# Moving the sample heads' means, two pieces of GpSimd's work and a table load inside one stage of a hybrid recurrent decoder step

## The chip, the cores and the metric

The kernel runs on one core of one Trainium2 chip, as a single launch. The metric is the time of that launch in microseconds on the device, taken as the median of several runs. TensorE is called PE here, VectorE DVE, ScalarE ACT, GpSimd POOL and SyncE SP, as in the profile. Each engine works through its own list of instructions in order; between engines there are only semaphores.

## The reference, cut to what matters

Two layers run over 320 tokens: a prompt of 256 and 8 samples of 8 tokens. Each layer is a SwiGLU feed-forward, a mixer, and a second feed-forward, with a layer norm after each. Half of the mixer's columns go to RWKV-7 heads, half to four mLSTM heads. The change lies in the mixer, where these two pieces meet:

```python
# mLSTM, per chunk of a sequence: C is the matrix memory, n the normaliser
num = g_inter[..., None] * jnp.einsum('bhtd,bhde->bhte', qc, C) + jnp.einsum('bhts,bhse->bhte', s, vc)
den = g_inter * jnp.einsum('bhtd,bhd->bht', qc, n) + s.sum(-1)
h = num / jnp.maximum(jnp.abs(den), jnp.exp(-m_t))[..., None]
C = dec[..., None, None] * C + jnp.einsum('bhs,bhsd,bhse->bhde', ws, kc, vc)
...
mu = h.mean(-1, keepdims=True)
var = jnp.mean(jnp.square(h - mu), -1, keepdims=True)
h = ((h - mu) * lax.rsqrt(var + MH_EPS)).reshape(B, T, D_B).astype(dt) * mh_g

# RWKV-7, per token: S is the matrix state
S = (S * w_t[:, :, None, :] + sa[..., None] * (kk_t * a_t)[:, :, None, :]
     + v_t[..., None] * k_t[:, :, None, :])
```

## The kernel before

The RWKV recurrence is done in chunks of 64 tokens: four of the prompt and one that holds all samples. Each chunk needs the inverse of a triangular matrix, which is grown in doublings. The stage that does this has 27 **steps** (`NSTEP`), numbered n, each a pair of a doubling level and a chunk. In a step PE makes a product, DVE masks it into `t1` (L1726, "the mask of step n"), PE makes the growth from it (L764 and L767), and ACT copies the growth back (L1183). After the last step the recurrence over the chunks begins, which needs every growth.

The mLSTM heads' work is threaded through the same 27 steps by hand: lists of step numbers say after which step each engine does which piece (`SIDE_AT`, `WEIGHTS_AT`, `NUMS_OUT_AT`, `SQUARES_AT`, `ROOTS_AT` for ACT; `PRODUCTS_AT`, `MEANS_AT`, `SPREADS_AT`, `SCALED_AT` and `LEFT_AT` for DVE; `LEFT_AT` for PE as well). There is no planner. What an engine has listed first it does first, and waits at it if it has to.

The pieces that the change and the prediction touch:

- `own_queries` (L1474, DVE): four products of two tiles in SBUF, two after step 16 and two after step 17. `tile_products` (L1482) is another such product.
- `inter_sums` (L1508) and `head_means` for the prompt, g=0 (L1533 to L1541), after step 17. The latter subtracts the mean from each head's row; its last instruction, L1541, reads two tiles of SBUF.
- `copy_nums` (L1125, ACT, after step 19) brings the sample heads' sums from PSUM to SBUF. `head_means` for the samples, g=1, waits for it: L1530, then L1533 to L1541.
- `head_squares` (L1139) and `head_roots` (L1147) on ACT. The roots need a table of ACT's that is loaded by `preload_act_table_set` (L1275).
- `head_spreads` (L1550 to L1556) and `head_scaled` (L1562 to L1566) on DVE. L1564 and L1566 read two tiles of SBUF.
- `left_over` on PE and `left_over_done` on DVE: thirteen units u=0 to 12 over three banks of PSUM. Eight are updates of the samples' matrix memory ("memory updates", C0 to C7: PE L648, DVE L1578 with four instructions each), three turn the prompt's and samples' heads (H0 to H2: PE L457 and L458, DVE L1584), one is the normaliser (N). PE's unit u waits until DVE is done with unit u-3, and DVE's list sets when that is. Units 0 and 1 belong to step 20, then two a step to step 24, H2 to step 25, N to step 26.
- POOL's list in this stage: `bkh` products (to L1940), a memset of `qm` (L1946), four DMAs of the samples' RWKV state (L1953), the diagonal decays (L1957, four products), `masked_values` for the first two heads (L1896, one product, g=0), the same for the other two (g=1), then four times `memory_term` (L1904, two products each). Memory term 1 waits for `hvar_ready` of the prompt's heads, memory term 3 for `left_mm` 10, that is for PE's unit 9 (C7), and memory term 2 for `hvar_ready` of the samples' heads, in that order.

`vmask[0]`, which the first `masked_values` writes, lies over `bkh` in `spare`; that is why it waits for the last copy that reads `bkh`. The decays overwrite `row`, whose last reader on PE is `gate_columns` (`cols_turned`); in the kernel before they wait for a later event, `tile_mm`.

Of the kernel before, what the change touches and what calls it, by code (L numbers as in the profile page):

```python
# [44 lines left out]
def hymba_kernel(nc, I, O):  # L45
# [3 lines left out]
    SB, ST, _ = I["x_sample"].shape  # L49
# [3 lines left out]
    HB, DK = I["state_C"].shape[2:4]  # L53
# [22 lines left out]
    NTT = 3  # L76
# [21 lines left out]
    with ExitStack() as ctx:  # L98
        def sb(name, shape, dt=F32):
            return ctx.enter_context(nc.sbuf_tensor(name, shape, dt))  # L100

        def signal(name, n, head=0):
            return Signal(ctx.enter_context(nc.semaphore(name)), n, head)
# [14 lines left out]
        spare = sb("spare", [P, 2 * KT * T])  # L118
# [38 lines left out]
        def area(at, *dims, rows=P, of=scratch):  # L157
            n = math.prod(dims)
            assert at + n <= of.shape[1], (at, dims)
            v = of[0:rows, at:at + n]  # L160
            if len(dims) == 1:
                return v
            names = " ".join(f"d{i}" for i in range(len(dims)))
            return v.rearrange(f"p ({names}) -> p {names}", **{f"d{i}": d for i, d in enumerate(dims)})
# [92 lines left out]
        qh = area(20424, HB, P)  # L257
        inter = area(27720, 36)
        hsq = area(0, 2 * HB * DK, of=spare)
        vmask = [area(1536, SB, DK, of=spare), area(15304, SB, DK)]  # L260

        s0 = area(12744, SB, NJ, NA)
        s0sum = area(14792, NJ, 2, TS)
# [78 lines left out]
        cols_turned = signal("cols_turned", 1)  # L342
# [5 lines left out]
        tile_mm = signal("tile_mm", NTT)  # L348
# [33 lines left out]
        side_copied = signal("side_copied", 19 - (NCH + 1) // 2)  # L382
# [282 lines left out]
        VALUES, KEYS, RVS, ENDS, MEMS = 1, 1 + NCH, 1 + 2 * NCH, 4 + 2 * NCH, 5 + 2 * NCH  # L665
# [5 lines left out]
        def copied_by_scalar(k):  # L671
            return k - (NCH + 1) // 2 if k >= KEYS else 1 + max(0, k - VALUES) // 2
# [400 lines left out]
        def copy_keys(act, L, n):  # L1073

            rows = TT[n][1]
            act.wait_ge(kv_turned.sem, kv_turned.by(L, n + 1))
            for h in range(HB):
                last = act.activation(kt[0:rows, n, h, :], bank[4 + n][0:rows, h * DK:(h + 1) * DK], ACT.Identity,
                                      scale=cols[0:rows, n, 1, h:h + 1])
            if n == 2:  # L1080
                for h in range(0, HB, 2):
                    last = act.activation(kt[PART[1], 2, h, :], bank[6][PART[1], h * DK:(h + 1) * DK], ACT.Identity,
                                          scale=cols[PART[1], 2, 1, h:h + 1])
            last.then_inc(kv_ready.sem, 1)

        def copy_values(act, L, n):

            rows = TT[n][1]
            act.wait_ge(kv_turned.sem, kv_turned.by(L, NTT + n + 1))
            if n == 2:  # L1090
                act.activation(va[PART[1], 2, 0:HB:2, 0:DK],
                               bank[5][PART[1], :].rearrange("p (h d) -> p h d", h=HB)[:, 0:HB:2, :], ACT.Copy)
            act.activation(va[0:rows, n, :, 0:DK], bank[(7, 4, 5)[n]][0:rows, :].rearrange("p (h d) -> p h d", h=HB),
                           ACT.Copy).then_inc(kv_ready.sem, 1)
# [8 lines left out]
        def output_gains(act, L, first, last):  # L1103

            for h in range(first, last):
                gained = act.activation(og[:, h, :], og[:, h, :], ACT.Identity, scale=vec[:, V_MH + h:V_MH + h + 1])
            if last == HB:
                gained.then_inc(og_ready.sem, 1)

        def tile_weights(act, L, n):  # L1110

            rows = TT[n][1]
            act.wait_ge(tile_mm.sem, tile_mm.by(L, n + 1))
            if n:
                act.activation(rexp[:, 0:HB * rows], bank[5][:, 0:HB * rows], ACT.Exp)
            act.wait_ge(wlog_ready.sem, wlog_ready.by(L, n + 1))
            act.activation(wexp[0:rows, :, 0:rows], wexp[0:rows, :, 0:rows], ACT.Exp).then_inc(wexp_ready.sem, 1)

        def copy_nums(act, L, n):

            rows = TT[n][1]
            act.wait_ge(num_mm.sem, num_mm.by(L, n + 1))
            if n == 2:
                for q, part in enumerate(PART):
                    last = act.activation(num[0:TS, n, q:HB:2, :], bank[4][part, 0:2 * (DK + 1)].rearrange(  # L1125
                        "p (h d) -> p h d", h=2), ACT.Copy)
                last.then_inc(num_ready.sem, 1)
                return
            act.activation(num[0:rows, n, 0:3, :], bank[4][0:rows, 0:3 * (DK + 1)].rearrange("p (h d) -> p h d", h=3),
                           ACT.Copy)  # L1130
            act.activation(num[0:rows, n, 3, :], bank[5][0:rows, 0:DK + 1], ACT.Copy).then_inc(num_ready.sem, 1)
# [45 lines left out]
        def copy_growth(act, L, n):  # L1177

            lv, c = LEVELS[n]
            act.wait_ge(x_mm.sem, x_mm.by(L, n + 1))  # L1180
            for q in range(2):
                rows = slice(0, P) if lv < NLV[c] - 1 else PART[1 - q]
                last = act.activation(xx[rows, c, q, :, :].rearrange("p j s -> p (j s)"),   # L1183
                                      bank[growth_bank(n) + q][rows, 0:NJ * CH], ACT.Copy)
            last.then_inc(x_copied.sem, 1)
# [64 lines left out]
        def scalar_mixers(act, L, split_hi):  # L1250

            act.drain()
            output_gains(act, L, 0, 2)
            for n in range(NTT):
                copy_keys(act, L, n)
            for n in range(NTT):
                copy_values(act, L, n)
                if n == 0:
                    output_gains(act, L, 2, HB)
            act.preload_act_table_set("natural_log_exp_and_others")  # L1260
            for n in range(NSTEP):
                if n < NCH:
                    copy_growth(act, L, n)
                if n in SIDE_AT and SIDE_AT.index(n) not in range(VALUES, KEYS, 2):
                    copy_side(act, L, SIDE_AT.index(n))
                if n in WEIGHTS_AT:
                    tile_weights(act, L, WEIGHTS_AT.index(n))
                if n >= NCH:
                    copy_growth(act, L, n)
                if n in NUMS_OUT_AT:  # L1270
                    copy_nums(act, L, NUMS_OUT_AT.index(n))
                if n in SQUARES_AT:
                    head_squares(act, L, SQUARES_AT.index(n))
                if n == SQUARES_AT[0] + 1:
                    act.preload_act_table_set("sqrt_and_others")  # L1275
                if n in ROOTS_AT:
                    head_roots(act, L, ROOTS_AT.index(n))
            scalar_recurrence(act, L, split_hi)

        WEIGHTS_AT = (4, 9, 14)  # L1280
        NUMS_OUT_AT = (7, 12, 19)
        SQUARES_AT = (17, 20)
        ROOTS_AT = (19, 22)


        def flat(t):
# [414 lines left out]
        def vector_mixers(dve, L, split_lo):  # L1701
# [19 lines left out]
            for n in range(NCH, NSTEP):  # L1721
# [14 lines left out]
                if n == INTER_AT:  # L1736
                    inter_sums(dve, L)
                if n in MEANS_AT:
                    head_means(dve, L, MEANS_AT.index(n))
                if n in SPREADS_AT:  # L1740
                    head_spreads(dve, L, SPREADS_AT.index(n))
                if n in SCALED_AT:
                    head_scaled(dve, L, SCALED_AT.index(n))
                for u in range(NLEFT):
# [6 lines left out]
        ADDED_AT = (8, 13)  # L1751
        QUERIES_AT = 17
        INTER_AT = 17
        MEANS_AT = (17, 20)
        SPREADS_AT = (19, 21)
        SCALED_AT = (20, 23)

        def make_identity(pool):
            pool.memset(ident[:, :], 0.0)
# [132 lines left out]
        def masked_values(pool, L, g):  # L1892

            values = va[:, 2, 2 * g, 0:DK].rearrange("t (o e) -> t o e", o=1)
            own = bmask[:, :].rearrange("t (b o) -> t b o", o=1)
            pool.tensor_tensor(vmask[g], bcast(values, 1, SB), bcast(own, 2, DK),  # L1896
                               ALU.mult).then_inc(vmask_ready.sem, 1)
# [9 lines left out]
        def pool_mixers(pool, L):  # L1907
# [35 lines left out]
            last.then_inc(bkh_ready.sem, 1)  # L1943
            pool.drain()
            pool.wait_ge(kv_ready.sem, kv_ready.by(L, 2 * NTT))
            pool.memset(qm[:, :, :], 0.0).then_inc(qm_zero.sem, 1)  # L1946
            pool.drain()
            pool.wait_ge(tail_out.sem, tail_out.by(L, 32))
            carry(pool)
            for a, part in enumerate(PART):  # L1950
                for q in range(2):
                    src = lay(I["state_wkv"]).rearrange("l b (j h) v k -> v (l b j) h k", h=4)
                    dma(wkv_rows[part, :, :, q * NA:(q + 1) * NA].rearrange("p b j k -> p (b j) k"),  # L1953
                        src[:, :, 2 * a + q, :]).then_inc(wkv_in.sem, 16)
            pool.wait_ge(tile_mm.sem, tile_mm.by(L, NTT))
            for j in range(NJ):
                pool.tensor_tensor(decay[:, :, j, :], bcast(id64[:, :].rearrange("p (o t) -> p o t", o=1), 1, SB),  # L1957
                                   bcast(dlast[:, j, NPC:NPC + SB].rearrange("p (b o) -> p b o", o=1), 2, NA),
                                   ALU.mult)
            pool.drain()  # L1960
            pool.wait_ge(side_copied.sem, side_copied.by(L, copied_by_scalar(RVS)))
            masked_values(pool, L, 0)
            pool.wait_ge(num_mm.sem, num_mm.by(L, NTT))
            masked_values(pool, L, 1)
            pool.drain()
# [975 lines left out]
```

## Time and profile before

| | |
|---|---|
| median of three runs | 1522.2 us (1518.78 to 1522.57) |
| the profiled execution's own time | 1519.59 us |
| its span in the trace | 1517.9 us |
| mean granted clock of PE | 0.986 |
| stage of 27 steps, layer 0 | about 393 to 459.5 us |
| stage of 27 steps, layer 1 | about 1137 to 1203.5 us |

The profile gives every instruction's start and duration, and for an engine that stood idle the instruction that released it. The two layers run the same code; the second stands some 744 us after the first. Times in the rows are us from the span's start, and the times of the working are those of layer 0.

### The profile page before, as it was taken

How to read it: one execution, taken by the hardware profiler on the slowest of the kernel's cores; microseconds unless marked ns; L12 is line 12 of the kernel's file. 1: busy time of each engine (PE TensorE's matmuls, PEld its weight loads, DVE VectorE, ACT ScalarE, POOL GpSimd, SP SyncE). 2: the span in 40 equal slices, each digit the busy share in tenths (PEclk: the TensorE clock that was granted, in tenths of full speed). 3: DMA queues.
4: the chain of work that ended last, by engine and by line, in shares of the span. 5: the costliest groups of instructions: out<-in, count | busy, mean ns of one | idle time of the engine just before them, and what ended most of it. 6: DMA issues, size and time to landing. Idle time of an engine off the chain costs nothing.

```text
span 1517.9 us, 33992 instructions
## 1 busy us (share of the span) xinstructions
PE 1464.3 (96%) x13374; PEld 1409.3 (93%) x13374; DVE 985.0 (65%) x1579; ACT 695.9 (46%) x1188; POOL 378.2 (25%) x407
## 2 busy tenths in 40 slices
PE   7999999999989999999999999989999899999995
PEld 7999998899867999999999999979998689999995
DVE  4444435588476687775577776466865777877644
ACT  5333334765645543334443334366565465333332
POOL 4222363010532422220412222300115323222100
PEclk9999999999999999999999999999999999999998
DMA  8544543443214555444544545434521444555351
GB/s 221 150 144 149 168 149 88 126 128 101 55 34 134 157 160 151 146 141 150 159 137 142 151 152 156 152 88 123 129 78 33 123 121 136 165 150 167 126 166 35
DMA packets 318938, 198.82 MB, mean 131 GB/s; under 512 B 7792, under 2 KB 303760, under 8 KB 318832
## 3 DMA queue, kind: packets, MB, share of 16 engines
q1 hardware_dynamic: 315120, 190.69, 43.1%
q0 software_dynamic: 3712, 6.62, 2.1%
q8 instruction: 78, 1.28, 0.3%
q14 instruction: 28, 0.23, 0.0%
HBM read 188.50 MB, written 8.78 MB: 130 GB/s over the span
## 4 chain that ended last, share of the span: by engine, by line
PE 85%; DVE 7%; ACT 3%; issue 2%; DVEq 1%; DMA 0%; POOL 0%; SPq 0%; POOLq 0%; ACTq 0%
PE bank L2120 24%; PE bank L2122 23%; PE bank L2121 23%; DVE wlo L2613 2%; PE bank L2207 1%; DVE rlo L2644 1%; ACT whi L2410 1%; ACT z L1183 1%; PE bank L2212 1%; PE bank L764 1%; PE bank L752 1%; DVE raw L1578 1%; PE bank L2171 1%; PE bank L853 1%; PE bank L458 1%
## 5 line engine op out<-in xcount | busy, mean ns | idle before, releaser
L2410 ACT ACTIVATE whi<-raw 128x1024 fp32r<-128x1024 f32 x340 | 358.2, 1059 | 471.9 <-PE bank L2122 455.7
L2613 DVE TENSOR_TENSOR wlo<-raw,whi 128x1024 fp32r<-128x1024 f32 x340 | 421.2, 1243 | 230.1 <-ACT whi L2410 229.3
L2120 PE MATMUL bank<-rhi,whi 128*128 128x322 f32 x984 | 306.5, 311 | 0.0
L2122 PE MATMUL bank<-rhi,wlo 128*128 128x322 f32 x984 | 305.9, 311 | 0.0
L2121 PE MATMUL bank<-rlo,whi 128*128 128x322 f32 x984 | 304.8, 310 | 0.0
L2120 PE MATMUL bank<-xh,whi 128*128 128x320 f32 x912 | 286.2, 314 | 4.6 <-DVE xl L2787 3.5
L2121 PE MATMUL bank<-xl,whi 128*128 128x320 f32 x912 | 283.0, 310 | 0.0
L2122 PE MATMUL bank<-xh,wlo 128*128 128x320 f32 x912 | 282.9, 310 | 0.0
L2882 POOL TENSOR_TENSOR hl<-scratch,hh 128x320 f32 x88 | 146.9, 1669 | 495.4 <-DVE scratch L2734 379.7
L2120 PE MATMUL bank<-hh,whi 128*128 128x320 f32 (+1 forms) x704 | 218.4, 310 | 0.5 <-DVE wlo L2613 0.5
L2121 PE MATMUL bank<-hl,whi 128*128 128x320 f32 (+1 forms) x704 | 217.4, 309 | 0.0
L2122 PE MATMUL bank<-hh,wlo 128*128 128x320 f32 (+1 forms) x704 | 217.4, 309 | 0.0
L2121 PEld LDWEIGHTS bank<-rlo,whi 128*128 128x128 f32 x984 | 186.4, 189 | 0.0
L2120 PEld LDWEIGHTS bank<-rhi,whi 128*128 128x128 f32 x984 | 185.5, 189 | 0.0
L2122 PEld LDWEIGHTS bank<-rhi,wlo 128*128 128x128 f32 x984 | 185.5, 189 | 0.0
L2120 PEld LDWEIGHTS bank<-xh,whi 128*128 128x128 f32 x912 | 173.2, 190 | 9.8 <-issue 6.6
L2121 PEld LDWEIGHTS bank<-xl,whi 128*128 128x128 f32 x912 | 173.2, 190 | 0.5
L2122 PEld LDWEIGHTS bank<-xh,wlo 128*128 128x128 f32 x912 | 173.0, 190 | 0.0
L2120 PEld LDWEIGHTS bank<-hh,whi 128*128 128x128 f32 x704 | 132.4, 188 | 1.3 <-issue 1.0
L2121 PEld LDWEIGHTS bank<-hl,whi 128*128 128x128 f32 x704 | 132.4, 188 | 0.2
L2122 PEld LDWEIGHTS bank<-hh,wlo 128*128 128x128 f32 x704 | 132.4, 188 | 0.0
L2715 DVE TENSOR_TENSOR scratch<-bank,scratch 128x322 f32<-128x322 f32 x132 | 64.9, 492 | 71.3 <-PE bank L2122 64.0
(421 smaller groups left out, 1888.8 us busy)
## 6 DMA issues: line engine op xcount, KB each, us to landing
raw<-in_ffn_wg SPq DMA_DIRECT2D x88, 512.0 KB, 3.8
raw<-in_ffn_wu SPq DMA_DIRECT2D x88, 512.0 KB, 3.8
raw<-in_ffn_wd SPq DMA_DIRECT2D x88, 512.0 KB, 3.6
raw<-in_w_in SPq DMA_DIRECT2D x60, 512.0 KB, 3.8
raw<-in_w_out SPq DMA_DIRECT2D x16, 512.0 KB, 6.1
raw<-in_state_C SPq DMA_DIRECT2D x8, 512.0 KB, 6.1
out_s_C<-raw SPq DMA_DIRECT2D x8, 512.0 KB, 4.1
ring<-in_state_wkv POOLq DMA_DIRECT2D x8, 256.0 KB, 5.5
```

What stands on the lines that cost most here:

```text
L458: return pe.matmul(out, src, ident[0:rows, 0:rows], start=True, stop=True)
L752: last = pe.matmul(bank[n % 2][PART[1 - q], j * CH:(j + 1) * CH], ati[part, c, j, :], xi(q, c, j), start=True, stop=True)
L764: pe.matmul(bank[2 + q][PART[q], j * CH:(j + 1) * CH], xti(q, c, j), t1[PART[1 - q], c, j, :], start=True, stop=True)
L853: last = pe.matmul(bank[4 + j][part, b * NA:(b + 1) * NA], s0[part, b, j, :], decay[part, b, j, :], start=False, stop=(b == SB - 1), skip_ ...
L1183: last = act.activation(xx[rows, c, q, :, :].rearrange("p j s -> p (j s)"), bank[growth_bank(n) + q][rows, 0:NJ * CH], ACT.Copy)
L2120: pe.matmul(out, w_hi, hi, start=start, stop=False)
L2121: pe.matmul(out, w_hi, lo, start=False, stop=False)
L2122: return pe.matmul(out, w_lo, hi, start=False, stop=stop)
L2410: act.activation(whi[:, slot, :], raw[:, slot, :], ACT.Copy).then_inc(hi_ready.sem, 1)
L2613: dve.tensor_tensor(wlo[:, slot, :], raw[:, slot, :], whi[:, slot, :].bitcast(F32), ALU.subtract).then_inc(lo_ready.sem, 1)
L2715: dve.tensor_tensor(scaled, bank_of(L, f, d)[:, 0:T + 2], root, ALU.mult)
L2882: pool.tensor_tensor(at(hl), hval[:, k % 2, :], at(hh).bitcast(F32), ALU.subtract).then_inc(hl_done.sem, 1)
```

## The change

- The sample heads' means (`MEANS_AT`) go from step 20 to step 21, with their squares, roots, spread and scaling a step later too. Within step 20 DVE then does the prompt heads' scaling and the memory updates C0 and C1 first, and the means come after the mask of step 21.
- The square root's table is loaded after step 16's copy instead of step 18's.
- `vmask[0]` gets a place of its own, over the end of `bk`, and the first `masked_values` moves ahead of the memset of `qm`: on POOL it is now also ahead of the four DMAs.
- The decays wait for `cols_turned` instead of the last `tile_mm`, and the wait for the last `bkh` copy is gone.

No instruction is added or removed.

```diff
-        vmask = [area(1536, SB, DK, of=spare), area(15304, SB, DK)]
+        vmask = [area(9480, SB, DK), area(15304, SB, DK)]
...
-                if n == SQUARES_AT[0] + 1:
+                if n == WEIGHTS_AT[2] + 2:
                     act.preload_act_table_set("sqrt_and_others")
...
         WEIGHTS_AT = (4, 9, 14)
         NUMS_OUT_AT = (7, 12, 19)
-        SQUARES_AT = (17, 20)
-        ROOTS_AT = (19, 22)
+        SQUARES_AT = (17, 21)
+        ROOTS_AT = (19, 23)
...
-        MEANS_AT = (17, 20)
-        SPREADS_AT = (19, 21)
-        SCALED_AT = (20, 23)
+        MEANS_AT = (17, 21)
+        SPREADS_AT = (19, 22)
+        SCALED_AT = (20, 24)
...
             pool.wait_ge(kv_ready.sem, kv_ready.by(L, 2 * NTT))
+            masked_values(pool, L, 0)
             pool.memset(qm[:, :, :], 0.0).then_inc(qm_zero.sem, 1)
...
-            pool.wait_ge(tile_mm.sem, tile_mm.by(L, NTT))
+            pool.wait_ge(cols_turned.sem, cols_turned.by(L, 1))
             for j in range(NJ):
                 pool.tensor_tensor(decay[:, :, j, :], bcast(id64[:, :].rearrange("p (o t) -> p o t", o=1), 1, SB),
                                    bcast(dlast[:, j, NPC:NPC + SB].rearrange("p (b o) -> p b o", o=1), 2, NA),
                                    ALU.mult)
             pool.drain()
-            pool.wait_ge(side_copied.sem, side_copied.by(L, copied_by_scalar(RVS)))
-            masked_values(pool, L, 0)
             pool.wait_ge(num_mm.sem, num_mm.by(L, NTT))
             masked_values(pool, L, 1)
```

## Rows read from the trace of the kernel before

**Rows 1.** The page: busy time by engine, and the chain by engine.
```profile
PE 1464.3 (96%) x13374; PEld 1409.3 (93%) x13374; DVE 985.0 (65%) x1579; ACT 695.9 (46%) x1188; POOL 378.2 (25%) x407
...
PE 85%; DVE 7%; ACT 3%; issue 2%; DVEq 1%; DMA 0%; POOL 0%; SPq 0%; POOLq 0%; ACTq 0%
```

**Rows 2.** The chain that ended last, layer 0's stage: start, us, what.
```profile
434.85 1.28 ACT L1275
...
443.59 1.12 PE bank L648 x2
```

**Rows 3.** Timeline of DVE, layer 0: start, us, instruction, count, [idle before].
```profile
425.26 0.89 DVE L1482 TENSOR_TENSOR scratch<-scratch,ring 128x256 f32<-128x256 f32 x1
...
427.53 2.04 DVE L1474 TENSOR_TENSOR scratch<-scratch,ring 128x64 f32<-128x64 f32 x2
429.50 0.17 DVE L1508 TENSOR_TENSOR scratch<-bank,bmask 64x32 f32<-64x32 f32 x1
...
431.67 1.17 DVE L1541 TENSOR_TENSOR ring<-ring,scratch 128x1024 f32<-128x1024 f32 x1
...
437.81 0.91 DVE L1530 TENSOR_TENSOR ring<-ring,scratch 64x4 f32<-64x4 f32 x1 [1.57 <-ACT ring L1125]
...
440.76 0.20 DVE L1562 RECIPROCAL scratch<-scratch 128x8 f32<-128x8 f32 x1
...
442.42 2.15 DVE L1578 SCALAR_TENSOR_TENSOR raw<-raw,ring,bank 128x128 f32<-128x128 f32 x8
...
448.52 1.27 DVE L1584 TENSOR_TENSOR scratch<-bank,scratch 128x512 f32<-128x512 f32 x2
449.71 0.40 DVE L1726 TENSOR_TENSOR spare<-bank,lvmask 128x256 f32<-128x256 f32 x1
450.40 0.17 DVE L1562 RECIPROCAL scratch<-scratch 64x4 f32<-64x4 f32 x1 [0.28 <-ACT scratch L1147]
450.64 0.15 DVE L1564 TENSOR_TENSOR scratch<-scratch 64x4 f32<-64x4 f32 x1
...
451.48 2.14 DVE L1578 SCALAR_TENSOR_TENSOR raw<-raw,ring,bank 128x128 f32<-128x128 f32 x8
...
455.95 0.41 DVE L1726 TENSOR_TENSOR spare<-bank,lvmask 128x256 f32<-128x256 f32 x1
```

**Rows 4.** Timeline of POOL, layer 0.
```profile
405.38 1.17 POOL L1946 MEMSET scratch<- 128x1280 f32 x1
...
407.52 3.31 POOL L1953 DMA_DIRECT2D ring<-in_state_wkv  x4 [0.61 <-issue]
422.82 4.23 POOL L1957 TENSOR_TENSOR scratch<-id,scratch 128x512 f32<-128x512 f32 x4 [11.99 <-PE bank L579]
427.54 1.96 POOL L1896 TENSOR_TENSOR spare<-ring,bmask 128x1024 f32<-128x1024 f32 x1 [0.48 <-ACT scratch L1165]
...
436.66 2.04 POOL L1904 TENSOR_TENSOR scratch<-scratch,bmask 128x512 f32<-128x512 f32 x2 [2.06 <-ACT scratch L1170]
453.85 2.04 POOL L1904 TENSOR_TENSOR scratch<-scratch,bmask 128x512 f32<-128x512 f32 x2 [15.15 <-PE bank L648]
```

**Rows 5.** Timeline of ACT, layer 0.
```profile
430.96 0.66 ACT L1183 ACTIVATE z<-bank 128x256 f32<-128x256 f32 x2 [2.51 <-PE bank L767]
...
436.14 0.44 ACT L1170 ACTIVATE scratch<-bank 120x128 f32<-120x128 f32 x2
...
437.00 0.78 ACT L1125 ACTIVATE ring<-bank 64x258 f32<-64x258 f32 x2
```

**Rows 6.** Timeline of PE, layer 0.
```profile
427.95 0.63 PE L614 MATMUL bank<-scratch 128*64 128x8 f32 x8
...
450.06 1.13 PE L648 MATMUL bank<-scratch,ring 64*128 64x512 f32 x4
```

**Rows 7.** Busy time by stretch: engines, PE's granted clock, DMA share, GB/s.
```profile
437.00:448.00 11.00, 8.54 (x119) 5.24 (x117) 9.49 (x31) 3.81 (x11) 1.70 (x2) 0.87 0.05 12
```

**Rows 8.** L1530 in both layers: ns min/median/max.
```profile
L1530 DVE TENSOR_TENSOR ring<-ring,scratch x2: 905/905/905, 437.8 to 1181.8; 64x4 f32<-64x4 f32 x2
```

## The prediction

> **What bounds the kernel now.** I read the page first. PE is busy 96% of the span and carries 85% of the chain that ended last; DVE carries 7%, ACT 3% [rows 1]. So most of the kernel is a row of matmuls that this change doesn't touch, and what it can move lies in the two stages of 27 steps, where engines hand small pieces to each other. There the chain leaves PE: it goes through ACT's table load (434.85) and through PE's memory update at 443.59, which had waited for DVE [rows 2]. The timelines of that stage say why, engine by engine.
>
> DVE is what ends last from step 16 on. Three losses are to be seen [rows 3]. A product of 128x256 (L1482) takes 0.89 us at 425.26 while POOL makes its decays, 422.82 to 427.05 [rows 4]. A pair of 128x64 products (L1474) takes 2.04 us from 427.53; POOL's masked values run from 427.54 to 429.50 [rows 4], and DVE's next instruction starts at 429.50, just then. At 437.81 a 64x4 product (L1530) takes 0.91 us, in both layers to the nanosecond [rows 8]; POOL's memory term runs 436.66 to 438.70 [rows 4]. All three read two tiles of SBUF, and each is released when a product of POOL ends. Before L1530 DVE also stood idle 1.57 us for ACT's copy of the samples' sums (L1125) [rows 3]. From 437.81 to 455.95 DVE hardly stops, and PE's units wait for it.
>
> **The change part by part.** *Queries.* Masked values (1.96 us) and decays (4.23 us) leave DVE's way. The inter sums (L1508) then wait only for PE's L614, which ends at 428.58 [rows 6]: 428.63 for 429.50, so 0.87 us. From there to the end of the prompt's means (432.84) nothing changes [rows 3]: 431.97.
>
> *Where that POOL work goes.* The masked values stand where the memset starts (405.38), and so push the memset and the four DMAs 2.0 us back, 407.52 to 409.5 [rows 4]; they issue until 412.8, and what they load is first used after 436, behind L1170's copy [rows 5]. The memset is needed by L1474 at about 426. Both cost nothing while these 14 us of cover stand; without it the 2.0 us would be paid. The decays then run from 412.9 to 417.1. One DVE product with two inputs in SBUF (L1482 of the tile before) stands near; a decay takes 4.23/4 = 1.06 us, so the bounds are 0 and 1.06 us of loss a layer. I take 0.
>
> *Table load.* It goes from 434.85, where it stands in the chain and the next copy starts at 436.14 right behind it [rows 2, 5], to the idle 2.51 us before the copy at 430.96 [rows 5]. 1.28 us fit, so it costs nothing there; if step 16's copy slipped by more than 1.2 us it would be paid in part. The Trainium skill (ScalarE: Activation LUTs, "What ACT_TABLE_LOAD costs") gives a switch some 2.66 us with a drain. The trace shows 1.28 us and no more; by the page the sums' copy would gain 1.4 us more, and the load would stick out of its new idle time by 0.15.
>
> *The samples' sums.* Query gain and load make at most 0.87 + 1.28 = 2.15 us, at least 0.87. With the load gone, ACT's copy of growth 19 waits for PE, which waits for the copy of growth 18 (0.66 us [rows 5]); I take 2.15 - 0.66 = 1.5. The sums are there at 436.3 for 437.78, and the prompt's roots, next on ACT, at 436.5.
>
> *DVE from there.* It now does the prompt's scaling first. L1562 starts at 436.5 for 440.76. POOL's memory term 1 comes 0.87 to 1.5 us earlier too, and ends at 437.2 to 437.8; L1564 meets it and I count 0.4 us. From L1562 to C0 is 1.66 us (440.76 to 442.42 [rows 3]), so C0 starts at 436.5 + 1.66 + 0.4 = 438.55. From C0 to the mask of step 23 DVE works 7.29 us without a gap (442.42 to 449.71); into this the samples' means now fall, 2.95 us (437.81 to 440.76), less the 0.74 us by which L1530 is no longer held up (0.91 against some 0.17). The mask of step 23 starts at T = 438.55 + 7.29 + 2.21 = 448.05 for 449.71. So far the change gains 1.66 us a layer.
>
> *Step 24, and what the samples' scaling meets there.* Two memory updates hold DVE 2.07 us and a mask 0.33 us (451.48 to 455.95 is two pairs and a mask [rows 3]). After C4, C5 and the mask of step 24, L1562 starts at T + 2.73 and L1564 at T + 2.97 (0.24 later, as at 450.40 and 450.64). Before, the scaling stood ahead of C4 and C5, with POOL idle. Now POOL's memory term 3 comes in: it wakes when PE has done unit 9, at 453.85, 3.8 us after unit 6 began at 450.06 and so 3.25 after unit 7 [rows 4, 6]. Unit 7 may start when H0 is done, 0.5 us before the mask (448.52 + 0.67 against 449.71). POOL wakes at T + 2.75 to T + 2.9, some 0.1 to 0.2 us before L1564. The query at 427.53 had no better margin and was held for the whole product [rows 3, 4].
>
> If so, L1564 waits for POOL's first product, to about T + 3.8; L1566 behind it finds the second one begun and waits to T + 4.9; with 0.6 us of its own, C6 starts at T + 5.5 and the mask of step 25 at T + 7.6 = 455.65 for 455.95: 0.3 us a layer. Queued behind these two on DVE are C6, C7 and the mask; PE waits for all of them. Bounds: if POOL comes after L1566 began, nothing is lost, the mask stands at T + 5.88 = 453.93, and 2.0 us a layer remain; if it comes between, L1566 alone waits some 0.9 us, and 1.1 us remain. I take the first, by the margin.
>
> The Trainium skill (SBUF — State Buffer, "SBUF: two separate sides") says the same of two engines: a DVE operation with two inputs in SBUF and a GpSimd operation that reads SBUF take a shared port pair as an exclusive lock, and the one that starts first keeps it for its whole instruction. That rule speaks for the moves on POOL and against the move of the scaling; by the rows above the trace agrees.
>
> After the mask of step 25 the same work follows as before, and the recurrence is a chain through PE that shifts along. H2 waits for the scaling (T + 5.5 = 453.55) and is through at 454.65, ahead of the mask.
>
> **The sum.** Two layers of 0.3 us: 1519.59 - 0.6 = 1519.0 us. That execution lies 2.6 us under the median of the three runs; against that median the same change gives 1521.6.
>
> **The rivals.** *No meeting in step 24* (or one product only): 1519.59 - 4.0 = 1515.6, with one product 1519.59 - 2.2 = 1517.4. For it: the margin is 0.1 to 0.2 us, and PE's clock was down for part of the stretch (0.87 granted from 437 to 448 [rows 7]); PE at half speed in units 4 to 7 brings POOL late. Against it: three meetings of this kind in the rows, all lost by DVE.
>
> *PE's clock falls in the tail: slower.* Between 437 and 448 PE was granted 0.87 on average, 11 x 0.13 / 0.5 = 2.9 us at 1.2 instead of 2.4 GHz [rows 7], with the wait that ended at 443.59 in it. That fell where DVE set the pace. After the change PE's longer wait comes later, before H2. If the slow stretch comes with it, it lies on H2, N and the last growths, which PE sets: 2.9 us at half speed add up to 1.45 us. 0.3 - 1.45 = -1.15 a layer, 1519.59 + 2.3 = 1521.9. It decides once more than 0.3 us of the gain is lost, that is 0.6 us of PE's tail at half speed. Against it: the wait is shared out over two places.
>
> *The move doesn't remove the wait.* DVE would stand for the roots (436.5) as it stood for the sums. That is already in the sum, as idle time before L1562; it would cost more only if ACT's sums came no earlier, and then the 0.87 us alone is left: the masks stay where they were, 1519.6.
>
> **How the numbers follow.** Full meeting 0.45, one product 0.2, none 0.2, slow tail 0.1, no gain 0.05. 1519.0 is the first. From 1515.3 (none, and a little of the decays' side) to 1523 (the slow tail, or the full meeting at the level of the median) all but some 2 in 10 is held. 0.3%, about what a measurement of this kernel can tell from no change, is 4.6 us: no case reaches it by itself. The runs spread over 3.8 us, so that none-meeting can come out beyond it almost as often as not, and the one-product case now and then: faster 0.17. Slower 0.07, from the slow tail and the decays' bound. Same 0.76.
>
> **What would show it.** Right: L1474's second pair under 0.5 us, L1508 at PE's L614's end; the table load in ACT's idle time before 431; L1530 at 0.2 us; in step 24 L1564 or L1566 near 1 us beside L1904, and the next mask about as late as before. Wrong: those two at 0.15 and 0.68 us, and the growths' end some 2 us earlier; a DVE product blocked near 412; or a granted clock under 0.95 over the tail.

## The result, and the profile after

The kernel after took 1533.32 us, the median of 4 runs (1527.92 to 1535.44), against 1521.76 us (4 runs, 1518.78 to 1522.57): ratio 1.0067, 95% interval 1.0045 to 1.0088. It is slower by 0.67%, and lies outside the range. Ratios and their intervals are those on record; the two medians alone would give 1.0076. Its profiled execution is its fastest run: 1527.92 us, span 1526.2 us, 8.3 us longer than the span before.

On the page nothing stands out. Busy time by engine, and the chain by engine:

```profile
PE 1471.7 (96%) x13374; PEld 1417.5 (93%) x13374; DVE 983.1 (64%) x1579; ACT 695.9 (46%) x1188; POOL 378.5 (25%) x407
...
PE 84%; DVE 9%; ACT 3%; issue 2%; DVEq 1%; POOL 1%; DMA 0%; POOLq 0%; SPq 0%; ACTq 0%
```

Against [rows 1], PE is busy 7.4 us longer with the same 13374 matmuls, DVE 1.9 us less; the chain gives DVE two points more and POOL a first one. PE doing the same in more time points at its clock. So I cut each stage in two, by the first and last of its 54 copies of a growth (L1183) and the last matmul of L926. Growths, then recurrence:

| | layer 0 | layer 1 |
|---|---|---|
| before | 66.02 + 27.14 = 93.16 us | 65.57 + 27.05 = 92.62 us |
| after | 67.23 + 31.86 = 99.09 us | 68.63 + 27.74 = 96.37 us |
| difference | +1.21, +4.72 | +3.06, +0.69 |

The sum is +9.7 us; the rest of the span gave 1.4 back. Layer 0 lost its time in the recurrence, layer 1 in the growths: two causes.

**Layer 0's growths went nearly as forecast up to the mask of step 25.** They begin at 392.14 us, for 393.52 before, so 1.38 is added to a time to compare it with before. The timeline of DVE in the kernel after, layer 0 (start, us, instruction, count, [idle before]):

```profile
427.81 0.18 DVE L1508 TENSOR_TENSOR scratch<-bank,bmask 64x32 f32<-64x32 f32 x1 [0.94 <-PE bank L614]
...
437.68 2.15 DVE L1578 SCALAR_TENSOR_TENSOR raw<-raw,ring,bank 128x128 f32<-128x128 f32 x8
...
440.08 0.15 DVE L1530 TENSOR_TENSOR ring<-ring,scratch 64x4 f32<-64x4 f32 x1
...
447.21 0.41 DVE L1726 TENSOR_TENSOR spare<-bank,lvmask 128x256 f32<-128x256 f32 x1
...
450.17 0.15 DVE L1564 TENSOR_TENSOR scratch<-scratch 64x4 f32<-64x4 f32 x1
450.75 1.38 DVE L1566 TENSOR_TENSOR ring<-ring,scratch 64x512 f32<-64x512 f32 x1 [0.43 <-issue]
...
454.12 0.41 DVE L1726 TENSOR_TENSOR spare<-bank,lvmask 128x256 f32<-128x256 f32 x1
```

C0 begins at 437.68 + 1.38 = 439.06 (forecast 438.55), the mask of step 23 at 448.59 (448.05; before 449.71 in [rows 3]), the mask of step 25 at 455.50 (455.65; before 455.95). L1530 is down to 0.15 us from the 0.91 of [rows 8]. The table load lies in ACT's idle time, and of step 24's two operations one was held, L1566, beside POOL's memory term 3. The timelines of ACT and POOL:

```profile
427.35 1.28 ACT L1275 ACT_TABLE_LOAD   x1
```
```profile
450.55 2.49 POOL L1904 TENSOR_TENSOR scratch<-scratch,bmask 128x512 f32<-128x512 f32 x2 [14.10 <-PE bank L648]
```

In layer 1 of the same profile neither of the two was held:

```profile
1204.76 0.15 DVE L1564 TENSOR_TENSOR scratch<-scratch 64x4 f32<-64x4 f32 x1
1204.99 0.68 DVE L1566 TENSOR_TENSOR ring<-ring,scratch 64x512 f32<-64x512 f32 x1
```
```profile
1205.14 2.44 POOL L1904 TENSOR_TENSOR scratch<-scratch,bmask 128x512 f32<-128x512 f32 x2 [14.10 <-PE bank L648]
```

**But then PE's clock falls.** Busy time by stretch in the kernel after (length, busy time of PE, PEld, DVE, ACT, POOL, then PE's granted clock, DMA share, GB/s):

```profile
437.00:448.00 11.00, 9.08 (x174) 5.99 (x174) 10.45 (x35) 3.59 (x9) 0.00 (x0) 1.00 0.34 95
448.00:453.00 5.00, 4.06 (x79) 2.96 (x75) 4.50 (x15) 2.09 (x6) 2.45 (x3) 1.00 0.03 8
453.00:460.00 7.00, 5.76 (x70) 5.19 (x70) 2.67 (x11) 1.51 (x4) 2.60 (x4) 0.54 0.56 160
460.00:477.00 17.00, 16.84 (x337) 15.64 (x336) 6.38 (x18) 6.62 (x17) 3.56 (x6) 0.50 0.49 139
...
1166.00:1171.00 5.00, 4.96 (x40) 4.84 (x42) 0.31 (x1) 0.00 (x0) 0.28 (x1) 0.66 0.00 0
```

and the same two stretches of the kernel before:

```profile
453.00:460.00 7.00, 6.07 (x114) 4.86 (x112) 4.49 (x18) 2.66 (x7) 4.43 (x5) 1.00 0.54 152
460.00:477.00 17.00, 14.46 (x462) 13.12 (x459) 9.34 (x28) 8.79 (x25) 3.70 (x6) 1.00 0.50 143
```

The 0.87 of [rows 7] became 1.00, and where before had 1.00 stands 0.50, the lower level, 1.2 GHz. The trace's clock records put the fall at 453.5 us and its length at 23.9 us. In 17 us PE got through 337 matmuls for 462, with hardly a gap. That is 27% fewer, not half: before, PE was busy only 14.46 of the 17 us. The recurrence ran some 18 us at half clock (459.4 to 477.4) and took 4.72 us more, about 0.26 us for each of them. What PE did before it fell:

```profile
443.46 0.66 PE L457 MATMUL bank<-ident,ring 128*128 128x128 f32 x4 [1.82 <-DVE raw L1578]
...
452.28 1.07 PE L458 MATMUL bank<-ident,ring 64*128 64x64 f32 x8 [0.94 <-DVE ring L1566]
...
455.63 1.87 PE L657 MATMUL bank<-bmask,ring 64*128 64x8 f32 x8
```

It waited 1.82 us before H1 (L457) and 0.94 us before H2 (L458), for DVE. L657, already at half clock, takes 1.87 us; in the chain of before (layer 1), 0.98. The wait before H1 alone was not enough: in layer 1 PE waited the same 1.82 us before H1 and not before H2, and the clock fell for 3.4 us only (at 1211.3).

**In layer 1 a product of DVE took 4.11 us.** The timelines of DVE, POOL and PE in the kernel after (POOL's L1958 is L1957 of the kernel before):

```profile
1161.27 4.11 DVE L1482 TENSOR_TENSOR scratch<-scratch,ring 128x512 f32<-128x512 f32 x1
```
```profile
1161.78 4.50 POOL L1958 TENSOR_TENSOR scratch<-id,scratch 128x512 f32<-128x512 f32 x4
```
```profile
1166.04 0.49 PE L598 MATMUL bank<-ring 128*128 128x129 f32 x2 [2.55 <-DVE ring L1484]
```

This is L1482 of the middle tile; in the kernel before it took 0.68 us:

```profile
1156.74 0.68 DVE L1482 TENSOR_TENSOR scratch<-scratch,ring 128x512 f32<-128x512 f32 x1
```

The four decays, now here, begin 0.51 us after it and run back to back (1161.78, 1162.78, 1163.78, 1164.78; the last takes 1.50 for some 1.05 us). L1482 ends at 1165.38, 0.60 after the last decay's start: it got in only ahead of the last one. PE stood 2.55 us behind it, and then ran at 0.66 of its clock from 1166 to 1171. In layer 0 L1482 began at 410.55, 0.75 us ahead of the decays, and took 0.80.

**Time and clock over all runs.** Every run carries its mean granted clock, and the same program is faster when it is higher: a least-squares line through the last 35 runs of before falls by 6.1 us for each 0.01 of clock (earlier groups of 29 and 30 runs: 6.5). Which stretch gets the low level differs from run to run, so a profile is one draw. After's four clocks (0.982, 0.980, 0.974, 0.975) average 0.978, before's 29 runs 0.984: by that line (an estimate) some 4 of the 11.6 us go with the clock.

### The profile page after: what moved, and what is told of

Read it like the earlier page. It is cut to its first block, busy times and chain, and to the rows that moved or that the text cites. A ratio compares the mean times of both kernels' runs of the same rounds, so it can differ in the third digit from the quotient of the medians.

```text
span 1526.2 us, 33992 instructions
## 1 busy us (share of the span) xinstructions
PE 1471.7 (96%) x13374; PEld 1417.5 (93%) x13374; DVE 983.1 (64%) x1579; ACT 695.9 (46%) x1188; POOL 378.5 (25%) x407
## 4 chain that ended last, share of the span: by engine, by line
PE 84%; DVE 9%; ACT 3%; issue 2%; DVEq 1%; POOL 1%; DMA 0%; POOLq 0%; SPq 0%; ACTq 0%
PE bank L2119 24%; PE bank L2121 23%; PE bank L2120 23%; DVE wlo L2612 2%; PE bank L2206 1%; DVE raw L1578 1%; ACT whi L2409 1%; DVE rlo L2643 1%; PE bank L2211 1%; PE bank L752 1%; PE bank L458 1%; ACT z L1183 1%; PE bank L853 1%; PE bank L764 1%; PE bank L807 1%
```

## The experiments

**Theory.** Two parts cost, each on its own. The decays' new place lets them meet the middle tile's L1482, which loses up to 3.4 us and PE after it. The means a step later put PE's wait behind the last units, and the clock falls over the recurrence. **Rivals.** One part does it all; or the meeting in step 24 does it and the clock only follows. The experiments were run in three groups, each with its own runs of before (medians 1521.49, 1522.56 and 1523.33 us); kernels of different groups are compared here by their ratios.

### Undoing one part: decays_back, means_back, both_back

Each is the kernel after with one part, or both, undone.

```diff
 decays_back:
-            pool.wait_ge(cols_turned.sem, cols_turned.by(L, 1))
+            pool.wait_ge(tile_mm.sem, tile_mm.by(L, NTT))
 means_back:
-        MEANS_AT = (17, 21)
-        SPREADS_AT = (19, 22)
-        SCALED_AT = (20, 24)
+        MEANS_AT = (17, 20)
+        SPREADS_AT = (19, 21)
+        SCALED_AT = (20, 23)
 (SQUARES_AT and ROOTS_AT likewise; both_back has both edits)
```

> The changed kernel, but the decays wait for the last tile_mm again, as before the change. Theory (two meetings): the loss of some 11 us has two parts. In layer 1 the decays met L1482 of the middle tile, which took 4.11 us for 0.68, and PE's clock fell behind it; in layer 0 the samples' scaling met memory term 3 in step 24, PE waited ahead of H2, and its clock fell over the recurrence. With the decays back the first part goes: 4 to 5 us less than the changed kernel, 1525 to 1529, L1482 of the middle tile at 0.68 in both layers, L1482 and L1474 of the last tile slow again (0.9 and 0.7). Rival (only the means' step costs): same as the changed kernel, 1531 to 1535. Rival (only the decays cost): 1522 or less.

> The changed kernel, but the sample heads' means, squares, spread, roots and scaling stand at their old steps (20, 20, 21, 22, 23). Theory (two meetings): the scaling no longer meets memory term 3, PE doesn't wait ahead of H2, and its clock doesn't fall at the growths' end; the decays' meeting with L1482 stays, as often as it comes. 1521 to 1528, with clock falls only behind L1482. Rival (only the means' step costs): 1516 to 1520. Rival (only the decays cost): 1531 to 1535.

> The changed kernel with both back: means at their old step and decays behind the last tile_mm. Left of the change are the early masked values and the earlier table load. Theory (two meetings): nothing of the loss is left, and the two gains stay: growths' end 1 to 2 us earlier a layer, 1517 to 1520. Rival (the masked values' early place, ahead of the four DMAs, or the earlier table load costs): slower than before by 3 us or more, 1525 and up.

Measured, with both stages' growths + recurrence as above (layer 0; layer 1):

| | median us | ratio to before | growths + recurrence of the profiled run |
|---|---|---|---|
| decays_back | 1528.58 | 1.0035 [1.0018, 1.0052] | 67.05 + 31.88; 65.79 + 30.37 |
| means_back | 1529.02 | 1.0052 [1.0033, 1.0071] | 69.51 + 29.58; 68.33 + 29.50 |
| both_back | 1522.06 | 0.9998 [0.9983, 1.0013] | 65.17 + 29.07; 65.51 + 29.70 |

Both parts cost, each alone: against both_back, the later means 6.5 us and the early decays 7.0 us. What both_back keeps, the early table load and masked values, costs nothing clear of noise and gains nothing: the 1517 to 1520 us expected of it didn't come. Its growths end 0.85 us earlier in layer 0 and 0.06 in layer 1, and its recurrence runs partly at the lower level, as before's profiled run did not.

All runs, and not the profiles alone, tell the two costs apart. By mean times decays_back lies 5.9 us above before, at a mean granted clock of 0.977 for 0.984; means_back lies 7.4 us above, at 0.979. By the line of that group (6.5 us for each 0.01, an estimate) the clock goes with 4.5 of the 5.9 us, but with only 3.3 of the 7.4.

In decays_back the middle tile's L1482 took 0.68 us in both layers and the growths of layer 1 are as before. The loss is in the recurrence; the clock falls at 453.5 us for 23.9 us and at 1207.8 for 13.7. In means_back the growths lose 3.5 and 2.8 us; its clock fell not only behind L1482, as expected, but also in the recurrence (6.8 us at 471.5 and at 1219.0), and its time lies 1 us above the range. Timelines of DVE and POOL in means_back, layer 0:

```profile
411.01 4.12 DVE L1482 TENSOR_TENSOR scratch<-scratch,ring 128x512 f32<-128x512 f32 x1
```
```profile
411.51 4.51 POOL L1958 TENSOR_TENSOR scratch<-id,scratch 128x512 f32<-128x512 f32 x4
```

In its layer 1 L1482 took 4.36 us.

### Taking the step-24 meeting away: term3_later

The kernel after, with POOL's memory term 3 behind unit 10 instead of unit 9.

```diff
-            pool.wait_ge(left_mm.sem, left_mm.by(L, 10))
+            pool.wait_ge(left_mm.sem, left_mm.by(L, 11))
             memory_term(pool, L, 3)
```

> The changed kernel, but memory term 3 on POOL waits for PE's unit 10 (H2) instead of unit 9, so that it comes behind the samples' scaling. Theory (meeting in step 24): L1564 and L1566 of the samples take 0.15 and 0.68 us, C6 follows at once, PE's wait ahead of H2 is shorter, and its clock stays up through the recurrence: 3 to 6 us less than the changed kernel, 1527 to 1530; what is left is the decays' meeting. Rival (PE's wait comes from the means' step itself, not from POOL): the clock falls all the same, 1531 to 1535.

Measured: 1527.47 us, ratio 1.0030 [1.0017, 1.0043]. L1566 took 0.68 us in both layers (after: 1.38 in layer 0; decays_back: 1.37 and 1.38), so the meeting was real, and without it about half of the loss is gone. That is more than the 0.70 us of L1566; the mean clock of its ten runs is 0.982, for 0.978 of after, which by the line above goes with some 2.6 us (an estimate). How the one leads to the other isn't traced here. But that the clock would stay up with it gone was wrong in layer 0: it fell at 454.6 us for 17.1 us, with PE's waits before H2 and before L767 at 0.62 us each. Layer 1's L1482 was again held, 3.97 us, the decays 0.37 us behind it; layer 0's began 0.62 us ahead of them and took 0.68.

### Keeping the decays early, apart from L1482: decays_drained, decays_behind

Both start from means_back. One puts a drain of POOL behind each decay, the other starts the decays only when DVE has left the middle tile's weights (L1484).

```diff
 decays_drained:
                                    ALU.mult)
+                pool.drain()
-            pool.drain()
 decays_behind:
-            pool.wait_ge(cols_turned.sem, cols_turned.by(L, 1))
+            pool.wait_ge(tile_w.sem, tile_w.by(L, 2))
```

> The kernel with the means back at their old step (means_back), and a drain of POOL after each of the four decays instead of one after all. Theory (a burst of POOL keeps the port): where L1482 of the middle tile is still running when the first decay starts, DVE gets in only ahead of the last of POOL's products that follow each other; with a drain between them it gets in after the first, so L1482 takes at most some 1.7 us instead of 4.1 and PE's wait behind it falls from 2.4 to under 0.5 us: 1522 to 1527. Rival (one product blocks for its own length and DVE lost by chance): 4 us as often as without drains, 1526 to 1533.

> The kernel with the means back at their old step, and the decays waiting for tile_w 2, that is until L1482 and L1484 of the middle tile are done (about 412), instead of cols_turned. Neither the decays nor the samples' scaling now meets a product of DVE. Theory (two meetings, and PE's clock follows its waits): the growths' end comes 2 us earlier a layer than before; if the clock stays up behind it, 1516 to 1519; if a fall in the recurrence takes the gain back, 1519 to 1524. Rival (early POOL work costs wherever it stands): 1526 or more.

Measured: decays_drained 1522.45 us, ratio 0.9993 [0.9978, 1.0009]; decays_behind 1522.11 us, ratio 0.9992 [0.9982, 1.0003]. Against means_back (1.0052) the whole loss is back, with nothing changed but when the decays run: 0.60% for decays_behind, some 9 us by the ratios, 6.9 by the medians. DVE and POOL in decays_behind, layer 0:

```profile
410.59 0.68 DVE L1482 TENSOR_TENSOR scratch<-scratch,ring 128x512 f32<-128x512 f32 x1
```
```profile
411.95 4.04 POOL L1958 TENSOR_TENSOR scratch<-id,scratch 128x512 f32<-128x512 f32 x4 [1.00 <-DVE ring L1484]
```

In decays_drained layer 0 the two did overlap, and there POOL was held (1.55 us) and DVE was not:

```profile
411.30 0.68 DVE L1482 TENSOR_TENSOR scratch<-scratch,ring 128x512 f32<-128x512 f32 x1
```
```profile
411.33 1.55 POOL L1958 TENSOR_TENSOR scratch<-id,scratch 128x512 f32<-128x512 f32 x1
...
417.23 3.41 POOL L1958 TENSOR_TENSOR scratch<-id,scratch 128x512 f32<-128x512 f32 x3 [4.35 <-issue]
```

In its layer 1 they didn't overlap. The idle time behind the first decay was 4.35 us in layer 0 and 4.60 in layer 1, so no more than one decay stood beside L1482 there, and a row of decays parted by short drains wasn't tried. So it is the overlap that costs; whether drains would save DVE in one like means_back's isn't shown.

decays_behind leaves a question. Its growths end 1.76 and 0.70 us earlier than before's (64.26 and 64.87 us), and the time is the same: in the profiled run its recurrence ran at half clock for 17.1 us in each layer, from 456.7 and 1204.2.

### Work for PE inside its waits: fill_h2, fill_h1_h2

decays_back, with transposes of the identity on PE into a free bank, six ahead of H2; the second kernel has eleven ahead of H1 too. Nothing reads them.

```diff
                     if LEFT_AT[u] == n:
+                        if u in FILL:
+                            for _ in range(FILL[u]):
+                                pe.transpose(bank[(n + 1) % 2][:, 0:P], ident[:, :], ident[:, :])
                         left_over(pe, L, u)
...
+        FILL = {10: 6}                (fill_h1_h2: {5: 11, 10: 6})
```

> The changed kernel with the decays back (decays_back), and six transposes of the identity on PE ahead of H2, into a bank that no one uses then: about 0.9 us of filler, as long as PE's wait there. What they write is never read. Theory (PE's wait ahead of H2 makes its clock fall): the clock stays at 1.0 over the recurrence, which takes some 27 us again for 29 to 31; 1520 to 1523. Rival (the clock falls for what PE did well ahead, the wait of 1.82 us before H1 among it): the fall stays, 1527 to 1530. Rival (the fall is chance): as decays_back, with the fall in one layer or the other.

> As fill_h2, with eleven transposes more ahead of H0's turn partner H1, about 1.6 us, as long as PE's wait there. Theory (PE's waits between units 5 and 10 make its clock fall): no fall from step 22 into the recurrence in either layer, 1518 to 1522. Rival (the fall comes from the recurrence itself, whose small matmuls wait for DVE and ACT): falls within the recurrence stay, 1525 to 1530.

Measured: fill_h2 1518.95 us (5 runs), ratio 0.9977 [0.9958, 0.9995], 0.58% under decays_back by the two ratios, some 9 us; fill_h1_h2 1521.21 us, ratio 0.9987 [0.9977, 0.9998]. PE in fill_h2, layer 0: the transposes take 0.88 us, and 0.17 us of waiting are left. The added lines shift the numbers: L1570 here is L1566.

```profile
452.47 0.88 PE L967 MATMUL bank<-ident 128*128 128x128 f32 x6
453.51 1.07 PE L458 MATMUL bank<-ident,ring 64*128 64x64 f32 x8 [0.17 <-DVE ring L1570]
```

The same stretches of decays_back, then of fill_h2:

```profile
453.00:460.00 7.00, 5.74 (x72) 5.15 (x71) 2.55 (x11) 1.51 (x4) 2.59 (x3) 0.53 0.55 160
460.00:477.00 17.00, 16.84 (x336) 15.63 (x336) 6.42 (x19) 6.61 (x17) 3.45 (x6) 0.50 0.48 139
...
1211.00:1228.00 17.00, 16.39 (x408) 15.44 (x408) 8.17 (x24) 7.44 (x20) 1.90 (x3) 0.69 0.51 143
```
```profile
453.00:460.00 7.00, 5.34 (x84) 4.62 (x81) 3.90 (x15) 1.87 (x5) 4.25 (x4) 0.89 0.52 153
460.00:477.00 17.00, 16.44 (x388) 15.31 (x386) 7.36 (x21) 7.18 (x19) 3.14 (x6) 0.64 0.48 142
...
1211.00:1228.00 17.00, 15.22 (x424) 12.60 (x420) 9.80 (x31) 10.65 (x35) 0.00 (x0) 1.00 0.33 97
```

PE was given more to do and was done sooner. The clock was expected to stay at 1.00; it did over nearly all of layer 1's recurrence, but in layer 0 it still fell, at 458.5 us for 13.7 us. Over all runs the mean clock is 0.987, for 0.977 of decays_back, which by the line above goes with some 6.5 of the 9 us (an estimate). A part isn't the clock's: the transposes also part L1566 from POOL's term 3 (1.03 and 0.68 us, for 1.37 and 1.38), and the growths end 1.4 and 0.7 us sooner than in decays_back.

The eleven more of fill_h1_h2 brought nothing further, 0.9987 for 0.9977, and its clock fell in the profiled run too (6.8 us at 454.5, 3.4 at 471.6 and at 1208.9), where no fall was expected. So filling the wait before H1 as well isn't shown to be worth anything.

### Is it the clock? A control, and a kernel that beats both

before_fill_h2 puts the same six transposes ahead of H2 into the kernel before, where PE doesn't wait; before_fill puts eleven into its 1.92 us before C3. behind_fill is decays_behind with eleven ahead of C3 and five ahead of H1, where that kernel's PE waits; behind_fill_more adds nine where it doesn't.

```diff
 before_fill_h2:    FILL = {10: 6}
 before_fill:       FILL = {3: 11}
 behind_fill:       FILL = {3: 11, 5: 5}
 behind_fill_more:  FILL = {3: 11, 5: 5, 7: 3, 10: 6}
```

> The kernel before with the six transposes ahead of H2 alone, as in the kernel that gained 9.6 us by them. There PE doesn't wait ahead of H2 and the clock stays at 1.00 over the recurrence. Theory (they pay only by the clock over the recurrence): 1521 to 1524 us, no gain. Rival (they pay by something else): 1512 to 1516 us.

> The kernel before with eleven transposes ahead of C3, inside PE's wait of 1.92 us there. Theory: the wait shrinks to 0.7 us; the clock's fall of 3.4 us at 445 and 1189, which lay in a stretch bound by DVE, goes away or moves. Gone: 1520 to 1523 us, since it cost nothing there. Moved into the recurrence: 1523 to 1527 us. Rival (any wait filled is time gained): under 1519 us.

> This is the kernel after with the means back at steps 17 and 20 and the decays begun after the middle tile's weights, plus transposes of the identity on PE ahead of C3 (eleven) and of H1 (five), where that kernel's PE waited 1.87 us and 0.89 us in each layer. Theory (the gain of the growths, 1.8 and 0.7 us earlier than before, is given back because PE's waits between steps 21 and 22 are followed by 17.1 us of half clock over the recurrence): both waits shrink under 0.7 us, the growths end where they did in the kernel without filler, the clock stays at 1.00 over at least one layer's recurrence, and the time is 1517 to 1520 us against 1522 for the kernel before. Rival (the clock over the recurrence is not set by what PE does in steps 21 to 22): 1522 us, the clock still falls at 456 and 1204.

> The kernel with eleven transposes ahead of C3 and five ahead of H1, plus three ahead of C5 and six ahead of H2, where PE had no wait to fill. Theory: the added nine cost at most 0.9 us a layer where the growths are bound by PE and nothing where they are bound by DVE, and the clock over the recurrence is no worse: 1517 to 1521 us. Rival (more work on PE always helps): under the kernel with sixteen.

| | median us | ratio to before | growths + recurrence of the profiled run |
|---|---|---|---|
| before_fill_h2 | 1525.06 | 1.0012 [1.0000, 1.0024] | 66.66 + 29.94; 66.23 + 29.41 |
| before_fill | 1523.05 | 1.0001 [0.9989, 1.0014] | 66.24 + 32.05; 66.02 + 28.97 |
| behind_fill | 1519.34 | 0.9979 [0.9966, 0.9991] | 65.25 + 28.33; 64.25 + 27.72 |
| behind_fill_more | 1526.10 | 1.0021 [1.0007, 1.0035] | 67.92 + 30.31; 67.35 + 28.35 |

The transposes are worth nothing by themselves: where PE has no wait, before_fill_h2 is 0.12% slower, at the edge of its interval, and behind_fill_more 0.42% behind behind_fill. In before_fill_h2 the clock was expected to stay at 1.00 over the recurrence, and in layer 0 of its profiled run it fell at 457.5 us for 13.7. In behind_fill_more the growths end 2.7 and 3.1 us after behind_fill's, where I had put the nine at 0.9 us a layer at most. Placed in decays_behind's waits, sixteen of them make a kernel 0.21% faster than before, where decays_behind shows no change; the step between the two, 0.13%, is not clear of their intervals. In behind_fill both waits shrank under 0.7 us, and the profiled run's falls to 3.4 us in each layer. Two stretches of decays_behind, then of behind_fill:

```profile
460.00:477.00 17.00, 16.78 (x384) 15.86 (x384) 7.37 (x22) 6.89 (x19) 0.81 (x2) 0.59 0.40 116
...
1204.00:1211.00 7.00, 7.00 (x154) 6.38 (x152) 1.97 (x5) 1.92 (x3) 3.90 (x6) 0.52 0.60 178
```
```profile
460.00:477.00 17.00, 14.60 (x467) 13.54 (x465) 9.24 (x27) 9.04 (x25) 1.90 (x3) 0.98 0.48 141
...
1204.00:1211.00 7.00, 5.67 (x189) 5.44 (x187) 2.61 (x7) 3.40 (x8) 1.91 (x3) 0.93 1.03 302
```

These two profiles lie further apart than the kernels do: their clocks are 0.981 and 0.990, where the means over all twelve runs are 0.983 and 0.985.

behind_fill has the early masked values, table load and decays of the change, the means where they were, and the filler. Beside fill_h2 it has the lowest ratio here.

before_fill shows the limit. It filled the wait that goes ahead of before's fall of the clock at 445 us; in its profiled run layer 0's fall came at 456.1 instead, for 20.5 us, over the recurrence, behind a wait of 0.89 us before H1 that before didn't have. Its median is that of before all the same. Which wait makes the clock fall when isn't settled by these runs: with a wait filled the fall came elsewhere, and only its price at the new place tells what filling was worth.

## Why the prediction was wrong

**Right, by the rows after.** The queries' gain: L1508 now waits for PE's L614 alone. The table load: hidden. L1530: 0.15 us. The sums, C0 and the mask of step 23 to 0.5 us, the mask of step 25 to 0.15 us. That last agreement is luck: layer 0 reached the mask of step 23 0.54 us late, and made it up because in step 24 the one-product rival came and not the full meeting. L1566 was held, L1564 was not; in layer 1 neither was. term3_later shows that the meeting costs.

**Failed: "a decay takes 4.23/4 = 1.06 us, so the bounds are 0 and 1.06 us of loss a layer. I take 0."** The loss isn't bounded by one decay: it reached the length of the row up to the last. L1482 lost 4.11 - 0.68 = 3.4 us, with the decays at 1161.78 right behind its start; PE's wait of 2.55 us came out of it. [rows 3] and [rows 4] held a hint and no more: the L1482 at 425.26 began during the third decay and got in ahead of the fourth, which fits a hold by one decay as well as a hold up to the last. The place was foreseen (the decays began at 411.30 + 1.38 = 412.68 for 412.9, beside the middle tile's L1482); the price was not. Priced by means_back against both_back, this step costs 7.0 us over both layers.

The Trainium skill (SBUF — State Buffer, "SBUF: two separate sides") lets the operation that starts first keep the port pair for its whole instruction. The trace doesn't bear that out here as its start times are recorded: in the profiles of after, means_back and term3_later L1482 began 0.37 to 0.75 us ahead of the first decay, six times, and lost four of them (3.97 to 4.36 us; leads 0.37, 0.50, 0.51 and 0.75). With leads of 0.62 and 0.75 it was left alone (0.68 and 0.80 us), so the lead by itself doesn't decide. Layer 0 of decays_drained does agree: L1482 began 0.03 us ahead and POOL's product was the one that was held.

**Failed: "the recurrence is a chain through PE that shifts along".** It shifts, but not at the same speed. The rival that had this, the clock's fall in the tail, was given 0.10 and 2.9 us at half clock a layer; the profiled run had 23.9 us in layer 0, and the recurrence lost 4.72 us where the rival had 1.45. The rival put a short fall on H2, N and the last growths, at 0.5 us for each us at half clock. The fall was long and lay on the recurrence, where a us at half clock cost less: in the seven recurrences of these profiles with 13 us or more of it, the loss against before's recurrence is 0.25 to 0.27 us for each. I had measured the fall's length where it happened to be short, beside a stretch that DVE bound. Priced by decays_back against both_back, the means' later place costs 6.5 us, and the filler ahead of H2 takes that and more back. Both signs, a DVE product blocked near 412 and a low clock over the tail, stand in the prediction as what would show it wrong.

**The sum** by the two prices would be 1522.1 (both_back) + 6.5 + 7.0 = 1535.6 us; 1533.3 was measured. In the profiled run layer 0 escaped the first cost, and layer 1 most of the second; whether the other three runs had both in both layers wasn't seen, as they have no profile.

**Open.** What decides the place and the length of the clock's fall. The waits before H1 and H2 go ahead of it, and filling the one before H2 shortened it. But both_back, with no wait of PE there in layer 0 (1.64 us before C3 instead), and decays_behind, with 0.89 us before H1 alone (and 1.87 before C3), also ran part of the recurrence at the lower level, and before_fill moved the fall there.

## What to carry to other kernels

Bound a meeting of a DVE product with a row of POOL products by the whole row, and start such a row with a wait on the DVE instruction that it would meet: one changed wait was worth 7 us here. Read the granted clock of the stretch behind an edit as well as that of its own: the 2.5 us that decays_behind's profiled run gained in a stretch bound by DVE were lost again in a chain of small matmuls that then ran at 1.2 GHz, and after lost more than it had gained. Where PE waits ahead of such a chain, a handful of matmuls that nobody reads can pay for themselves. Outside a wait they cost, inside one they don't always pay (before_fill gained nothing), and one profile isn't enough to judge it by.

## What the hardware showed that I had not expected

- A DVE product with two inputs in SBUF, begun 0.37 to 0.75 us ahead of four back-to-back POOL products, was four times let in only ahead of the last: 3.97 to 4.36 us for 0.68, and the last POOL product took 1.50 us for 1.05. Twice, with leads of 0.62 and 0.75 us, it was not held. Begun 0.03 us ahead of a single one that had a drain behind it, it took 0.68 us and POOL 1.55.
- At the lower level the recurrence stayed busy and stayed there: 16.84 us busy of 17 at 0.50, until 477.4 us, with matmuls nearly without a gap. Some 18 us of it at half clock took 4.72 us longer than before, a quarter and not half.
- Six transposes of 128x128, 0.88 us of work that nothing reads, made decays_back some 9 us faster (0.58%) where PE waited, and the same six in the kernel before, where it didn't wait, gained nothing (1.0012).
